# One fixed load order on the sync queue, modulation weights by halves, and attention heads transposed per 128 tokens as each is ready

## Chip, cores, metric

One Trainium2 chip; the kernel runs on one of its cores. The metric is the device time of one execution in microseconds (us): the median of three runs, and beside it one profiled execution of its own.

## What is computed

A slice of a diffusion backbone with two layers over 256 latent tokens and 256 context tokens, width 1024, all in float32. Every layer takes six modulation vectors from a conditioning vector (6 x 1024 columns of `mod_w` per layer), mixes tokens, normalises, sends the tokens through a grouped mixture of 16 experts (two chosen per token) and normalises again. Layer 0 mixes by differential attention, layer 1 by pooling:

```python
ml = (jax.nn.silu(c) @ mod_w[i] + mod_b[i])[:, None, :]
sh1, sc1, g1, sh2, sc2, g2 = jnp.split(ml, 6, axis=-1)
hl = xl * (1.0 + sc1) + sh1
# layer 0, per block of 128 query tokens, 8 heads, two score maps per head
s = jnp.einsum('bqhnd,bkhnd->nbhqk', qb, k) * scale
p = jax.nn.softmax(s, axis=-1)
a = p[0] - lam_full * p[1]
o = jnp.einsum('bhqk,bkhe->bqhe', a, v)
o = o * lax.rsqrt(jnp.mean(jnp.square(o), axis=-1, keepdims=True) + LN_EPS)
yl = (o * subln * (1.0 - lam_init)).reshape(B, Lq, D_MODEL) @ wo
xl = deepnorm_update(xl, yl, g1, ln_g[i, 0], ln_b[i, 0])
y2 = moe_ffn(tokens, router_w, router_b, moe_wg[i], moe_wu[i], moe_wd[i])
xl = deepnorm_update(xl, y2, g2, ln_g[i, 1], ln_b[i, 1])
```

## The kernel before, in words

The program is written out by hand for every engine; semaphores order it. Each engine, and each of the queues that issue loads, works through its own list in order.

**Memory.** The largest buffer is `ring`: ten slots of 128 x 4096 floats, 2 MB each. An expert takes six slots (two each of `moe_wg`, `moe_wu`, `moe_wd`), and the ring is refilled in the order of FREE while experts run. Before the experts the same slots hold weights of the attention, tokens, keys, values, queries and heads. A unit is 2 MB of weights, 1024 x 512.

**Ahead of the experts.** PHASE_A is the order in which PE uses its units: four modulation units ("mod", 0, 2, 1, 3), then ("k", j), ("q", j), ("v", j) for two halves j of the heads, then ("wo", 0) and ("wo", 1). `half_group` (first half of the contraction, then second) and `group` multiply one of twenty groups of GROUPS; groups 10 to 19, those of j = 1, come one per attention step through FILL.

The other twenty modulation units (SUMS, NSUM = 20) are summed on DVE: `unit_sum(n)` is two calls of `half_sum`, eight instructions that multiply a 128x512 piece by a column of the conditioning and add it into `sums` (the first L1269, six L1271, the last L1273). They pass through ring slots 2 and 3 in turn. EARLY_SUMS = 8 units are summed before the first attention step, with `rope_batch` (L1307 to L1310) before unit 6 and after unit 7; STEP_SUMS = 10 come one per step, the last two behind the attention. `row_batch(b)` on PE (L592) takes four finished sums.

**Steps.** There are NS = 16 attention steps, one per (half j, 128 tokens t, head h) in STEPS. In step s PE multiplies a filling group (s = 1 to 9), does the scores of step s (`scores`, L685), turns the weights of step s-2 (`turn_probs`, L538) and multiplies values of step s-3 (`values`, L703). DVE takes the maximum of the scores (L1391, L1392), combines the two maps of the step before (L1397, L1398, L1402), and sums a unit. ACT does the exponentials (L1096), copies the turned weights (L1100) and the results (L1105, L1107). PE waits in `scores(s)` for the exponentials of s-1, and these wait for DVE's maximum.

**Heads.** After the steps DVE normalises the heads of each 128 tokens (`norm_heads(t)`, L1322 to L1329) between two ACT pieces, `heads_std(t)` (L1077, a square root) and `copy_heads(t)` (L1084); between these PE turns the heads (`turn_heads(t)`, L538), and then multiplies by the output weights (`project(t, h)`, L722). `job(3)`, `job(4)` (L744) and `row_batch(4)` stand among them. Then come the first normalisation and the routing, and the experts begin (L862).

**Queues.** The sync queue (SP; every load is at L414) carries the attention weights and after them the experts' units. Its list waits for what frees a slot: `load_early` by FREED_BY, `slot_free(v)` for the first ten experts' units. The modulation units of SUMS come through the queue of GpSimd (POOL, L518), 2 MB at a time:

```python
for n, (layer, m) in enumerate(SUMS):
    s = 2 + n % 2
    if n < 2:
        pool.wait_ge(sem("unit_used"), s - 1)
        pool.wait_ge(sem("early_loaded_6"), 16)
    else:
        pool.wait_ge(sem("summed"), n - 1)
    pool.dma_start(slot(s), mod_w[layer, m]).then_inc(sem(f"sum_loaded_{n % 2}"), 16)
```

ACT's own queue swaps halves of keys and queries for the rotation (L1034, eight loads of 128 KB from ring to ring per half j).

## Time and profile before

| | us |
|---|---|
| runs (3) | median 1250.11, lowest 1246.59, highest 1251.18 |
| profiled execution | 1251.67 |
| its span | 1249.8 |
| PE busy | 1139.6 (91%) |
| DVE busy | 357.7 (29%) |
| ACT busy | 165.4 (13%) |
| POOL busy | 15.9 (1%) |

The span runs from the first to the last recorded instruction; the profiled execution took 1.87 us more than it. All positions below are microseconds from the start of the span. PE runs the matmuls, PEld its weight loads, DVE the vector work, ACT the activations; a name with q (SPq, ACTq) is a queue that issues loads. The loads themselves run on 16 DMA engines, which moved 480.17 MB, 384 GB/s in the mean. The program writes every float32 matmul as one instruction and the profile counts two.

### The profile page before, as it was taken

The numbers are of one execution on the slowest core, as the hardware profiler recorded it, in microseconds if no ns is written. First come the engines' busy times: TensorE is split into PE (matmuls) and PEld (weight loads), VectorE is DVE, ScalarE is ACT, GpSimd is POOL, SyncE is SP. The second block draws the span as 40 slices with busy tenths as digits, with TensorE's granted clock in tenths as the row PEclk, the third lists the DMA queues.
The fourth block names the chain that finished last, engine by engine and source line by source line (L and its number), as shares of the span: only waits on it lengthen the run. The fifth ranks groups of instructions, "written<-read, shape, count | busy, mean of one in ns | idle before, by whom it ended". The sixth has DMA issues, their size and how long they took to land.

```text
span 1249.8 us, 12318 instructions
## 1 busy us (share of the span) xinstructions
PE 1139.6 (91%) x5288; PEld 510.1 (41%) x5288; DVE 357.7 (29%) x729; ACT 165.4 (13%) x398; POOL 15.9 (1%) x28
## 2 busy tenths in 40 slices
PE   8995998888999999999999898899999999999995
PEld 3552464535444334333333336543333334333331
DVE  1458889764111112111111104211111111111113
ACT  1110223524100001000000003301000000100000
POOL 0000000000000000000000001000000000000000
PEclk9997999789999999999999999899999999999998
DMA  9997596937799999999999999799999999999993
GB/s 395 403 337 256 216 329 268 394 145 303 318 429 427 428 428 427 428 427 427 427 428 428 427 420 426 311 428 427 427 429 428 427 427 428 427 427 428 428 427 156
DMA packets 37273, 480.17 MB, mean 384 GB/s; under 512 B 4704, under 2 KB 5984, under 8 KB 8032
## 3 DMA queue, kind: packets, MB, share of 16 engines
q1 hardware_dynamic: 33280, 434.96, 82.7%
q0 software_dynamic: 2880, 41.94, 8.9%
q10 hardware_dynamic: 1056, 2.43, 0.6%
q8 instruction: 44, 0.72, 0.2%
q14 instruction: 13, 0.11, 0.0%
HBM read 476.18 MB, written 1.05 MB: 382 GB/s over the span
## 4 chain that ended last, share of the span: by engine, by line
PE 70%; DVE 14%; DMA 11%; issue 3%; ACT 2%; SPq 0%; DVEq 0%; POOLq 0%
PE ps L862 51%; DMA ring<-in_mod_w 7%; PE ps L854 5%; PE ps L870 5%; DMA ring<-in_moe_wu 3%; DVE ring L1271 3%; PE ps L722 2%; DVE work L1594 2%; DVE modp L1271 1%; DVE work L1598 1%; PE ps L878 1%; DVE extra L1271 1%; DVE small L1391 1%; PE ps L622 1%; PE ps L538 1%
## 5 line engine op out<-in xcount | busy, mean ns | idle before, releaser
L862 PE MATMUL ps<-ring,tra 128*64 128x512 f32 x2048 | 446.7, 594 | 2.2 <-ACT tra L1149 1.1
L862 PEld LDWEIGHTS ps<-ring,tra 128*64 128x64 f32 x2048 | 145.9, 137 | 298.1 <-issue 294.0
L862 PE MATMUL ps<-ring,work 128*64 128x512 f32 x1024 | 228.5, 598 | 29.2 <-DVE work L1594 29.2
L862 PEld LDWEIGHTS ps<-ring,work 128*64 128x64 f32 x1024 | 83.2, 137 | 153.8 <-issue 117.4
L1589 DVE TENSOR_TENSOR work<-ps,work 128x512 f32<-128x512 f32 x32 | 22.1, 692 | 277.8 <-ACT work L1156 277.8
L1156 ACT ACTIVATE work<-ps 128x512 f32<-128x512 f32 x32 | 19.1, 597 | 535.1 <-PE ps L862 535.1
L870 PE MATMUL ps<-work,extra 64*128 64x512 f32 x256 | 63.6, 615 | 21.0 <-DVE work L1598 21.0
L1149 ACT ACTIVATE tra<-ps,cols 128x128 f32<-128x128 f32 x128 | 48.2, 456 | 245.3 <-PE ps L854 245.3
L854 PEld LDWEIGHTS ps<-extra,xn 128*128 128x128 f32 x512 | 63.8, 203 | 25.7 <-issue 22.7
L1592 DVE TENSOR_TENSOR work<-work,ps 128x512 f32<-128x512 f32 x32 | 22.0, 688 | 181.4 <-PE ps L862 181.4
L854 PE MATMUL ps<-extra,xn 128*128 128x128 f32 x512 | 69.5, 293 | 2.7 <-DVE extra L1502 2.7
L622 PE MATMUL ps<-ring 128*128 128x512 f32 x128 | 58.2, 609 | 0.7 <-ACT ring L1045 0.7
L870 PEld LDWEIGHTS ps<-work,extra 64*128 64x128 f32 x256 | 22.0, 186 | 61.4 <-DVE work L1598 46.3
L1598 DVE TENSOR_TENSOR work<-ps,gt 128x512 f32<-128x512 f32 x16 | 11.1, 692 | 117.0 <-PE ps L862 117.0
L1598 DVE TENSOR_TENSOR work<-ps,rows 128x512 f32<-128x512 f32 x16 | 11.1, 691 | 115.3 <-PE ps L862 115.3
L622 PEld LDWEIGHTS ps<-ring 128*128 128x128 f32 x128 | 24.5, 195 | 33.6 <-issue 33.5
L1594 DVE COPY work<-ps 128x512 f32<-128x512 f32 x32 | 22.1, 692 | 50.8 <-PE ps L878 50.8
L1271 DVE SCALAR_TENSOR_TENSOR ring<-ring,cols 128x512 f32<-128x512 f32 x48 | 36.1, 752 | 1.7
L1096 ACT ACTIVATE work<-ps,small 128x512 f32<-128x512 f32 x32 | 21.7, 683 | 72.6 <-DVE small L1392 72.6
L628 PE MATMUL ps<-ring 128*128 128x256 f32 x128 | 30.1, 396 | 1.3 <-DMA ring<-in_attn_wqkv 1.3
L625 PE MATMUL ps<-ring 128*128 128x512 f32 x64 | 28.1, 592 | 0.0
L563 PE MATMUL ps<-cst 128*128 128x512 f32 x44 | 23.7, 670 | 4.3 <-DMA cst<-in_consts 4.0
(186 smaller groups left out, 752.4 us busy)
## 6 DMA issues: line engine op xcount, KB each, us to landing
ring<-in_moe_wg SPq DMA_DIRECT2D x64, 2048.0 KB, 25.0
ring<-in_moe_wu SPq DMA_DIRECT2D x64, 2048.0 KB, 23.4
ring<-in_moe_wd SPq DMA_DIRECT2D x64, 2048.0 KB, 23.1
ring<-in_mod_w POOLq DMA_DIRECT2D x20, 2048.0 KB, 9.6
ring<-in_mod_w SPq DMA_DIRECT2D x4, 2048.0 KB, 18.4
ring<-in_attn_wqkv SPq DMA_DIRECT2D x4, 2048.0 KB, 13.8
ring<-in_attn_wo SPq DMA_DIRECT2D x2, 2048.0 KB, 10.6
ring<-in_tokens SPq DMA_DIRECT2D x2, 1024.0 KB, 16.2
```

What stands on the lines that cost most here:

```text
L563: mm(bank(bk), ident, cst[:, 0:NB], start=True, stop=True, skip_group_check=True)
L622: return mm(bank(acc_bank(g)), w[:, k, t * P:t * P + P], hT[:, k, :], start=first, stop=end)
L625: return mm(bank(acc_bank(g)), hT[:, k, t * P:t * P + P], rhs, start=first, stop=end)
L628: last = mm(bank(acc_bank(g), 0, P, n * TOK, (n + 1) * TOK), w[:, k, hd * P:hd * P + P], hT[:, k, 0:TOK], start=first and n == 0, stop=end ...
L722: last = mm(bank(2 * t + h), oT[t][:, k, :], wo[:, k, :], start=(k == 0), stop=(k == KT - 1))
L854: last = mm(bank(bk, 0, P, k * P, k * P + slots), xn[:, c0:c0 + P], sgat[:, t, 0:slots], start=(t == 0), stop=(t == TT - 1), skip_group_ch ...
L862: last = mm(ps[SLOTS * h:SLOTS * h + SLOTS, b, :], lhs(k0 + k), w[:, k, h * NB:(h + 1) * NB], start=(k0 + k == 0), stop=(k0 + k == KT - 1) ...
L870: last = mm(bank(2 * t + h), sw[SLOTS * h:SLOTS * h + SLOTS, t * P:t * P + P], ysb[SLOTS * h:SLOTS * h + SLOTS, :], start=False, stop=True ...
L1149: nc.scalar.activation(xg[i // 2 % 2][:, kk, :], bank(bk, k * P, k * P + P), ACT.Identity, bias=one(bcol[2 * layer], kk, 1), scale=one(aco ...
L1271: link(v_.scalar_tensor_tensor(out=acc, in0=w[:, k, :], scalar=ck, in1=acc, op0=ALU.mult, op1=ALU.add))
L1594: v_.tensor_copy(work[:, NB:2 * NB], bank(7)).then_inc(sem("hTt_copied"), 1)
L1598: v_.tensor_tensor(ysb, bank(6), gt[layer], ALU.mult).then_inc(sem("ys_ready"), 1)
```

## The change

The SP queue gets one list, LOADS, for all weights ahead of the experts: an integer n is unit n of SUMS, loaded as two 1 MB halves; a pair is an attention unit; "rows" the router's weights and the bias rows; "x" the latent tokens. Each half waits for the sum of the same half two units earlier (the semaphore half_summed takes the place of summed). The POOL queue loads nothing any more. DVE waits per half. On DVE and ACT the heads of the first 128 tokens are normalised inside the last steps (s = NS-1 and NS+1), and PE turns them right behind `turn_probs(NS - 1)`; it turns those of the second 128 tokens ahead of `project(0, 1)`, with `job(4)` and `row_batch(4)` behind it.

```diff
+LOADS = [("q", 0), 0, 1, ("v", 0), 2, "rows", 3, 4, ("k", 1), 5, 6, 7, 8, ("q", 1), 9, 10, 11, 12, ("v", 1), 13, 14, ("wo", 0),
+         15, 16, 17, ("wo", 1), "x", 18, 19]
...
-            for unit in EARLY:
+            for unit in (("mod", 0), ("mod", 2), ("k", 0), ("mod", 1), ("mod", 3)):
                 load_early(unit)
...
+            def load_sum_unit(n):
+
+                layer, m = SUMS[n]
+                for half in range(2):
+                    if n >= 2:
+                        sp.wait_ge(sem("half_summed"), 2 * (n - 2) + half + 1)
+                    else:
+                        early_used(sp, ("mod", (0, 2)[n]))
+                    c0, c1 = half * UNIT // 2, (half + 1) * UNIT // 2
+                    load(slot(2 + n % 2)[:, c0:c1], mod_w[layer, m][:, c0:c1], sem(f"sum_loaded_{n % 2}_{half}"))
+
+            for what in LOADS:
+                if what == "rows":
+                    load_rows()
+                elif what == "x":
+                    load(xn[:, :].rearrange("p (t n) -> p t n", t=TT), x[0].rearrange("(t p) n -> p t n", p=P), sem("x_loaded"))
+                elif isinstance(what, tuple):
+                    load_early(what)
+                else:
+                    load_sum_unit(what)
...
                 elif v in (6, 7):
-                    sp.wait_ge(sem("summed"), NSUM - 7 + v)
+                    sp.wait_ge(sem("half_summed"), 2 * (NSUM - 7 + v))
...
-            for n, (layer, m) in enumerate(SUMS):
...
-                pool.dma_start(slot(s), mod_w[layer, m]).then_inc(sem(f"sum_loaded_{n % 2}"), 16)
...
                     values(NS - 3)
                     turn_probs(NS - 1)
+                    turn_heads(0)
                     values(NS - 2)
                     values(NS - 1)
                     job(3)
-                    turn_heads(0)
                     project(0, 0)
-                    job(4)
...
-            project(0, 1)
-            row_batch(4)
             pe.wait_ge(sem("aT_copied"), NS)
             pe.wait_ge(sem("o_copied"), NS)
             turn_heads(1)
+            project(0, 1)
+            job(4)
+            row_batch(4)
...
+                if s == NS - 1:
+                    heads_std(0)
                 if 2 <= s < NS + 2:
                     act.wait_ge(sem("aT_done"), s - 1)
                     nc.scalar.copy(aT[s % 2], bank(4)).then_inc(sem("aT_copied"), 1)
+                if s == NS + 1:
+                    copy_heads(0)
...
-                if half == 0:
-                    dve.wait_ge(sem(f"sum_loaded_{n % 2}"), 16 * (n // 2 + 1))
-                    if n >= SUM_BUFS:
-                        dve.wait_ge(sem("row_done"), (n - SUM_BUFS) // BATCH + 1)
+                dve.wait_ge(sem(f"sum_loaded_{n % 2}_{half}"), 16 * (n // 2 + 1))
+                if half == 0 and n >= SUM_BUFS:
+                    dve.wait_ge(sem("row_done"), (n - SUM_BUFS) // BATCH + 1)
...
-            norm_heads(0)
+                if s == NS - 1:
+                    norm_heads(0)
```

The SP queue behind the first units, before (`unit_used` counts units that PE is done with; 128x4096 is 2 MB, 128x2048 is 1 MB):

```order
L414 DMA cols<-in_attn_subln 128x1
L414 DMA ring<-in_attn_wqkv 128x4096 [waits unit_used]
L414 DMA xn<-in_attn_wqkv 128x2048
L414 DMA tra<-in_attn_wqkv 128x2048
L414 DMA rwa<-in_router_w 128x256
L414 DMA rb<-in_router_b 128x16
L414 DMA rows<-in_bias_rows 128x512 x2
L414 DMA pscale<-in_scale_rows 128x512
L414 DMA ring<-in_attn_wqkv 128x4096 [waits unit_used] x3
L414 DMA ring<-in_attn_wo 128x4096 [waits unit_used] x2
L414 DMA xn<-in_x 128x2x1024
L414 DMA ring<-in_moe_wg 128x4096 [waits unit_used]
```

And the same queue with the change, up to the loads behind ("q", 1):

```order
L417 DMA ring<-in_attn_wqkv 128x4096 [waits unit_used]
L417 DMA ring<-in_mod_w 128x2048 [waits unit_used] x4
L417 DMA xn<-in_attn_wqkv 128x2048
L417 DMA tra<-in_attn_wqkv 128x2048
L417 DMA ring<-in_mod_w 128x2048 [waits half_summed] x2
...
L417 DMA ring<-in_mod_w 128x2048 [waits half_summed] x4
L417 DMA ring<-in_attn_wqkv 128x4096 [waits unit_used]
L417 DMA ring<-in_mod_w 128x2048 [waits half_summed] x8
L417 DMA ring<-in_attn_wqkv 128x4096 [waits unit_used]
L417 DMA ring<-in_mod_w 128x2048 [waits half_summed] x8
```

The modulation halves now stand between the attention weights, and ("k", 1) behind the halves of unit 4.

PE at the end of the attention, before, from `values(NS - 2)` (the first L703 row) to the second projection of the first 128 tokens:

```order
L703 MATMUL ps<-ring,tra 128x128 [waits o_copied,qkv_out,aT_copied]
L703 MATMUL ps<-ring,tra 128x128 x3
L744 MATMUL ps<-rows,cst 128x512
L538 MATMUL ps<-cst,ring 128x128 [waits job_out,o_normed]
L538 MATMUL ps<-cst,ring 128x128 x7
L722 MATMUL ps<-ring,work 128x512 [waits oT_copied,early_loaded_1]
L722 MATMUL ps<-ring,work 128x512 x7
L744 MATMUL ps<-rows,cst 128x512 [waits job_out]
L722 MATMUL ps<-ring,work 128x512 [waits oT_copied,early_loaded_0]
L722 MATMUL ps<-ring,work 128x512 x7
```

And with the change, from `turn_heads(0)` on (L538 of ring are heads, L718 values, L737 the projections, L759 the jobs):

```order
L553 MATMUL ps<-cst,ring 128x128 [waits job_out,o_normed]
L553 MATMUL ps<-cst,ring 128x128 x7
L718 MATMUL ps<-ring,tra 128x128 [waits o_copied,qkv_out,aT_copied]
L718 MATMUL ps<-ring,tra 128x128 x3
...
L759 MATMUL ps<-rows,cst 128x512
L737 MATMUL ps<-ring,work 128x512 [waits oT_copied,early_loaded_1]
L737 MATMUL ps<-ring,work 128x512 x7
L553 MATMUL ps<-cst,ring 128x128 [waits o_normed,o_copied,aT_copied]
L553 MATMUL ps<-cst,ring 128x128 x7
L737 MATMUL ps<-ring,work 128x512 [waits oT_copied,early_loaded_0]
L737 MATMUL ps<-ring,work 128x512 x7
L759 MATMUL ps<-rows,cst 128x512 [waits job_out]
```

Both turns of heads moved up by one block of other PE work, and a job moved down.

## Rows read from the trace of the kernel before

**Rows 1.** Windows in the experts: window, busy us of each engine (instructions), clock, DMA share, GB/s
```profile
405.00:465.00 60.00, 58.10 (x282) 22.95 (x280) 9.94 (x21) 4.80 (x11) 0.00 (x0) 1.00 1.01 428
```
**Rows 2.** Waits of the SP queue, 285 to 345 us: total us, times, longest
```profile
SPq L414 <- PE ps L862: 45.8, 6, 26.5
```
**Rows 3.** Window between last load ahead of the experts and first refill, columns as rows 1
```profile
312.00:316.00 4.00, 3.44 (x20) 2.77 (x21) 1.36 (x7) 2.55 (x7) 0.00 (x0) 0.79 0.00 0
```
**Rows 4.** Chain that ended last, 0 to 330 us, shares by line
```profile
by line: DMA ring<-in_mod_w 27.6%; DVE ring L1271 9.7%; PE ps L722 9.2%; DVE modp L1271 5.5%; PE ps L862 4.2%; DVE extra L1271 4.2%; issue 3.6%; DVE small L1391 3.6%; PE ps L622 2.6%; PE ps L703 2.3%; PE ps L685 2.2%; PE ps L854 2.0%; PE ps
```
**Rows 5.** Timeline of DVE, 44 to 115 us: start, duration, what, [idle before <-releaser]
```profile
44.16 0.14 DVE L1299 TENSOR_SCALAR cols<-cols 128x1 f32<-128x1 f32 x1
...
89.02 0.49 DVE L1269 TENSOR_SCALAR ring<-ring,cols 128x512 f32<-128x512 f32 x1 [13.73 <-DMA ring<-in_mod_w]
...
99.37 0.49 DVE L1269 TENSOR_SCALAR ring<-ring,cols 128x512 f32<-128x512 f32 x1 [4.36 <-DMA ring<-in_mod_w]
...
108.82 0.48 DVE L1269 TENSOR_SCALAR ring<-ring,cols 128x512 f32<-128x512 f32 x1
...
114.73 0.48 DVE L1269 TENSOR_SCALAR ring<-ring,cols 128x512 f32<-128x512 f32 x1
```
**Rows 6.** Timeline of PE, 43 to 125 us
```profile
43.42 8.86 PE L628 MATMUL ps<-ring 128*128 128x256 f32 x32 [1.32 <-DMA ring<-in_attn_wqkv]
...
101.42 7.03 PE L622 MATMUL ps<-ring 128*128 128x512 f32 x16
120.77 1.93 PE L592 MATMUL ps<-ring,cst 128*32 128x512 f32 x8 [12.32 <-DVE ring L1273]
124.30 2.08 PE L685 MATMUL ps<-ring 64*128 64x512 f32 x4 [1.60 <-DVE ring L1310]
```
**Rows 7.** Timeline of PE in the steps: scores of steps 1, 2 and 10
```profile
134.87 1.13 PE L685 MATMUL ps<-ring 64*128 64x512 f32 x4
...
143.00 1.13 PE L685 MATMUL ps<-ring 64*128 64x512 f32 x4
...
214.28 1.13 PE L685 MATMUL ps<-ring 64*128 64x512 f32 x4
```
**Rows 8.** Timeline of DVE in the steps: maxima of 1, 2, 4, 10, and unit 12
```profile
136.05 1.23 DVE L1391 TENSOR_REDUCE small<-ps 128x2 f32<-128x1024 f32 x1 [2.21 <-PE ps L685]
...
144.41 1.22 DVE L1391 TENSOR_REDUCE small<-ps 128x2 f32<-128x1024 f32 x1
...
162.14 1.23 DVE L1391 TENSOR_REDUCE small<-ps 128x2 f32<-128x1024 f32 x1 [0.29 <-PE ps L685]
...
168.61 0.49 DVE L1269 TENSOR_SCALAR ring<-ring,cols 128x512 f32<-128x512 f32 x1 [3.94 <-DMA ring<-in_mod_w]
...
223.34 1.22 DVE L1391 TENSOR_REDUCE small<-ps 128x2 f32<-128x1024 f32 x1
```
**Rows 9.** Windows by the queues at work, columns as rows 1
```profile
11.00:22.00 11.00, 10.75 (x54) 4.54 (x46) 3.10 (x8) 1.76 (x4) 0.00 (x0) 1.00 0.99 418
...
66.00:98.00 32.00, 32.00 (x98) 16.66 (x97) 14.64 (x21) 3.58 (x7) 1.58 (x3) 1.00 0.99 325
```
**Rows 10.** Timeline of POOL: the first two loads of modulation units
```profile
34.26 1.25 POOL L518 DMA_DIRECT2D ring<-in_mod_w  x2 [33.80 <-DMA ring<-in_mod_w]
```
**Rows 11.** Timeline of ACT behind the steps: loading the square root's table
```profile
252.27 1.28 ACT L1077 ACT_TABLE_LOAD   x1
```
**Rows 12.** Timeline of PE behind the steps: projections, and the first expert
```profile
257.91 9.37 PE L722 MATMUL ps<-ring,work 128*128 128x512 f32 x16 [0.87 <-ACT work L1084]
...
278.04 13.97 PE L722 MATMUL ps<-ring,tra 128*128 128x512 f32 x32 [1.01 <-ACT tra L1084]
...
315.17 13.95 PE L862 MATMUL ps<-ring,tra 128*64 128x512 f32 x64 [0.56 <-ACT tra L1149]
```
**Rows 13.** Loads by kind, 0 to 300 us: count, KB each, median us to landing
```profile
cols<-in_cond SPq DMA_DIRECT2D x1, 8.0 KB, 2.7
```
**Rows 14.** Timeline of DVE behind the steps: normalising the first 128 tokens' heads
```profile
254.05 1.23 DVE L1329 TENSOR_TENSOR ring<-ring,small 128x1024 f32<-128x1024 f32 x1
```

More of the change, by code:

```diff
@@ L436, in load_early @@
                         load(slot(s)[:, c0:c1], src[:, c0:c1], sem("first_half_loaded" if part == 0 else f"early_loaded_{s}"))
-            for unit in EARLY:
+            for unit in (("mod", 0), ("mod", 2), ("k", 0), ("mod", 1), ("mod", 3)):
                 load_early(unit)
-                if unit == ("mod", 3):
-                    load(small9[:, 0:512], rope, sem("attn_small_loaded"))
-                    load(lamb, attn_lam[0].rearrange("a b -> (a b)").partition_broadcast(P), sem("attn_small_loaded"))
-                    load(subln, attn_subln.rearrange("a n -> n a"), sem("attn_small_loaded"))
-                if unit == ("v", 0):
-                    load(rw[:, :], router_w, sem("router_loaded"))
-                    load(rb[:, 0:NE], router_b.partition_broadcast(P), sem("router_loaded"))
-                    for i in range(DEPTH):
-                        load(rows[i][:, :], bias_rows[i], sem(f"rows_loaded_{i}"))
-                    load(pscale[:, :], scale_rows, sem("pscale_loaded"))
@@ L450, in _, with load_rows @@
-            load(xn[:, :].rearrange("p (t n) -> p t n", t=TT), x[0].rearrange("(t p) n -> p t n", p=P), sem("x_loaded"))
+            load(small9[:, 0:512], rope, sem("attn_small_loaded"))
+            load(lamb, attn_lam[0].rearrange("a b -> (a b)").partition_broadcast(P), sem("attn_small_loaded"))
+            load(subln, attn_subln.rearrange("a n -> n a"), sem("attn_small_loaded"))
+            def load_rows():
+                load(rw[:, :], router_w, sem("router_loaded"))
+                load(rb[:, 0:NE], router_b.partition_broadcast(P), sem("router_loaded"))
+                for i in range(DEPTH):
+                    load(rows[i][:, :], bias_rows[i], sem(f"rows_loaded_{i}"))
+                load(pscale[:, :], scale_rows, sem("pscale_loaded"))
@@ L510, in _ @@
         def _(pool):
-            for n, (layer, m) in enumerate(SUMS):
-                s = 2 + n % 2
-                if n < 2:
-                    pool.wait_ge(sem("unit_used"), s - 1)
-                    pool.wait_ge(sem("early_loaded_6"), 16)
-                else:
-                    pool.wait_ge(sem("summed"), n - 1)
-                pool.dma_start(slot(s), mod_w[layer, m]).then_inc(sem(f"sum_loaded_{n % 2}"), 16)
             pool.wait_ge(sem("job_out"), JOBS.index("joint_1") + 1)
@@ L584, in row_batch @@
             def row_batch(b):
-                pe.wait_ge(sem("summed"), BATCH * b + BATCH)
+                pe.wait_ge(sem("half_summed"), 2 * (BATCH * b + BATCH))
                 if b == SUMS0 // BATCH:
@@ L1107, in _ @@
                     nc.scalar.copy(osb[:, t, hh * P:hh * P + P], bank(5, 0, P)).then_inc(sem("o_copied"), 1)
-            for t in range(TT):
-                heads_std(t)
-                copy_heads(t)
+            heads_std(1)
+            copy_heads(1)
             def std(n, t):
@@ L1268, in half_sum @@
                     if k == 0:
-                        link(v_.tensor_scalar(acc, w[:, 0, :], ck, None, ALU.mult))
-                    elif k < KT - 1:
-                        link(v_.scalar_tensor_tensor(out=acc, in0=w[:, k, :], scalar=ck, in1=acc, op0=ALU.mult, op1=ALU.add))
-                    else:
-                        v_.scalar_tensor_tensor(out=acc, in0=w[:, k, :], scalar=ck, in1=acc, op0=ALU.mult, op1=ALU.add)\
-                            .then_inc(sem("summed"), 1)
+                        ins = v_.tensor_scalar(acc, w[:, 0, :], ck, None, ALU.mult)
+                    else:
+                        ins = v_.scalar_tensor_tensor(out=acc, in0=w[:, k, :], scalar=ck, in1=acc, op0=ALU.mult, op1=ALU.add)
+                    if k % 4 < 3:
+                        link(ins)
+                ins.then_inc(sem("half_summed"), 1)
+                if half == 0:
+                    dve.wait_ge(sem("half_summed"), i + 1)
             def unit_sum(n):
```

## The prediction

> **What bounds the kernel now.** I read the experts first, because they are most of the span. There PE is busy for 58.10 of 60 us while the loads run at 428 GB/s [rows 1]; PE sets the pace and the loads keep up. What matters for a change ahead of the experts is whether PE finds the ring full when it begins. It does: between 312 and 316 us nothing is loaded at all [rows 3], and the SP queue's longest wait there, 26.5 us, is for PE to give a slot back [rows 2]. The last slots to be filled come free with the output projections, at a fixed distance ahead of the first expert, so they move with it. From the first expert at 315.17 us [rows 12] everything is the same chain of work whenever it starts. So the change is worth the time by which that start moves, one for one.
>
> Next I read the chain of waits up to 330 us. Loads of `mod_w` are its largest part, 27.6%, with the sums on DVE behind them [rows 4]. The timelines show where it bites. Between units 3 and 4 of the sums DVE stood 13.73 us for a load, before unit 5 another 4.36, and before unit 12, in the steps, 3.94 [rows 5, 8]. PE had all its early groups done at 101.42 + 7.03 = 108.45, then stood 12.32 us for the eighth sum and 1.60 for the rotation behind it, and began the scores at 124.30 [rows 6]. From there to the maximum of step 10 at 223.34 DVE is the slower of the two: PE had those scores ready from 214.28 on [rows 7, 8].
>
> **The first 108 us.** The change removes twenty POOL loads of 2 MB and adds forty SP loads of 1 MB. What counts is when they land. An issue took 0.6 us of a sequencer (two took 1.25 [rows 10]); forty of them, 25 us, are spread over 170 us in a queue that waits most of that time, and I cost them at nothing. For the rate I take 420 GB/s, near the 418 of a stretch in which the SP queue was alone, several of its loads being of 1 MB [rows 9]: 5.0 us for 2 MB, 2.5 for a half. The last early unit had landed at 33.8 [rows 10]; with the small loads behind it the list begins to land at about 35. It then goes: q0 40, unit 0 45, unit 1 50, v0 55, unit 2 60, the small rows (0.9 MB) 62, unit 3 67, unit 4 72, k1 with ACT's eight swaps (1 MB) beside it 79.5, units 5, 6, 7 at 84.5, 89.5, 94.5.
>
> On DVE a sum takes 114.73 - 108.82 = 5.91 us, and 108.82 - 99.37 - 5.91 = 3.54 is a rotation [rows 5]. It is free at 44.3 [rows 5] and needs only first halves to start: units 0 and 1 end at 56.1, unit 2 starts with its first half at 57.5 and ends 63.4, unit 3 70.4, unit 4 76.3; unit 5 starts at 82 and ends 87.9, rotation 91.4, unit 6 97.4, unit 7 103.3, rotation 106.8. PE meanwhile gains the 1.32 us that it stood for q0 [rows 6] and has its groups done at 107.1; the four matmuls of `row_batch(1)` take 1.1 (1.93 at the lower clock [rows 6]). The scores begin at **108.2** instead of 124.30, **16.1 us** earlier, and now PE is last, by about 1 us only. If that cover is gone, each further microsecond on DVE counts in full.
>
> **The steps.** PE came out of its idle time slow: four score matmuls took 2.08 us where later ones took 1.13, and the step took 10.57 us (124.30 to 134.87) against 8.13 for the next (to 143.00) [rows 6, 7]. Without the idle time I give the first step 8.1: scores of step 1 at 116.3, their maximum 1.2 later at 117.5. From the maximum of step 1 to that of step 10 DVE took 223.34 - 136.05 = 87.3 us, of it 3.94 for unit 12's load and 0.29 for PE [rows 8]. Without the load wait 83.4 remain: step 10 at **200.9, 22.4 us** earlier. PE alone needs at most 214.28 - 134.87 = 79.4 [rows 7], which is 195.7, so DVE stays last.
>
> The new waits in the list do not bite here by this schedule. ("v", 1) waits for k1, which PE is done with at about 133, as DVE frees the last half of unit 12 at 134; DVE wants unit 13, behind it, in step 5, near 158. ("wo", 0) waits for q1, done near 153; unit 15 behind it is wanted near 178. ("wo", 1) waits until about 192, and behind it stand x, units 18 and 19, wanted behind the steps, and the first experts.
>
> **Behind the steps.** Before, ACT's table load began at 252.27, DVE's normalisation at 254.05, and the projection at 257.91 [rows 11, 12, 14]: 5.6 us with no other work on PE but job(3). Now ACT loads the table (1.28) in the last step, ahead of a copy that PE waits for, and DVE's 1.23 and two small ones stand ahead of the last weights. They push PE's last values by 1.5 to 2.9 us, and turning heads inside the sequence costs PE 1.1 or more. I work out 3.1 us added against 5.6 removed: 2.5 gained. The second turning is followed by other PE work, which saves the 1.01 us at 278.04 [rows 12]. Job(4), moved behind a projection, needs 0.7 us on DVE, hidden by `row_batch(4)`. Together **3.5 us**. The ends: 0, if ACT's and DVE's new work lies wholly on the path, and 5.8, if PE is also at the higher clock in the first projection (9.37 for it against 13.97 for two [rows 12]).
>
> **Sum.** 22.4 + 3.5 = 25.9 us off the profiled execution's 1251.67 gives 1225.8. The median of the runs was 1.56 lower: **1224.2**.
>
> **Rivals.**
>
> 1. *The rate stays low.* From 66 to 98 us the DMA engines were 99% busy and moved 325 GB/s, with three queues at work [rows 9]. If the cause is not the mixture of queues, it remains. The 18.7 MB from v0 to unit 7 then take 57.5 us from 50, the last half lands at 107.5, and 3.0 + 3.5 + 0.3 later the scores begin at 114.3: 6.1 us less gained, 1230.3. For it: ACT's swaps remain. Against it: 418 and 428 with one queue [rows 1, 9]. The Trainium skill, page DMA: Bandwidth & Descriptors, section Issuing engines are not separate DMA queues, says that loads from any engine run on the same 16 DMA engines and interleave, so merging queues would change order and not rate; by that rule the sum is this rival's. The rows bear it out only in part, since no stretch shows these loads on one queue.
>
> 2. *Part of the waits remains.* The list is in order, and one late weight holds all halves behind it. Half of DVE's 22.0 us of load waits [rows 5, 8] staying would give 1235.2. Against it are the margins above, except the 1 us at 108.2.
>
> 3. *Slower: halves do not overlap.* If each load waited for the one before to complete, a half would cost its 2.5 us and the 2.7 us that a small load took alone [rows 13], a unit 10.4. The place is the SP queue ahead of the steps and in them. Up to unit 7: 35 + 8 x 10.4 + 10.4 (v0) + 7.7 x 2 (q0, k1) + 15.7 (five small ones) = 159.7, then 6.8 on DVE: scores at 166.5, 42 later. In the steps, ten units and four weights take 134.8 against 99.0, another 36. With the 3.5 this is 1325. It decides where a unit takes longer than a step of 8.36 [rows 8], or 1.7 us lost per half. Against it: 418 GB/s in a stretch with 1 MB loads queued [rows 9]. The Trainium skill, page SBUF — State Buffer, section The DMA setup-cost knee, speaks against this change: every transfer pays roughly 2 us whatever its size, so transfers should be as large as they can be. With that figure a unit would be estimated at 9.0, still over a step; queued loads in the rows do not show it.
>
> 4. *Nothing moves*, if something unseen holds the steps; PE's 12.32 us of idle time speaks against it.
>
> **How the numbers follow.** Forecast 0.62; rival 1 0.20; rival 2 0.10; rival 3 0.03; rival 4 0.03; more than forecast 0.02. A measurement can tell 0.5%, 6.3 us, from no change. Forecast, rivals 1 and 2 and the surplus are faster by more: 0.94, same 0.03, slower 0.03. The range goes down by the tail's 2.3 us and 3.5 of spread (a run stood that far from the median) to 1218, and up past rival 1 with nothing gained behind the steps (1233.8) to 1236.
>
> **What would show it.** Right: POOL issues no loads; DVE waits little for loads but some 5 us before unit 5; PE goes without a long gap from 107 to the scores at about 108; the maximum of step 10 near 201, the first expert near 289; nothing loading just ahead of it. The rate from 66 to 98 us separates rival 1. A load wait of over 3 us on DVE in the steps would show rival 2, halves landing 5 us apart rival 3. A first expert at 289 with a total above 1235 would prove the reading of the experts wrong.

## The result, and the profile after

The changed kernel took 1230.09 us, the median of 4 runs (1228.50 to 1231.78), and the kernel before 1249.60 (4 runs, 1246.59 to 1251.18). The ratio is 0.984 (0.9823 to 0.9857), so the change gains 19.5 us where 25.9 were forecast for it. The profiled execution took 1231.51 us, 20.2 less than the 1251.67 before.

The page of the changed kernel, its parts 1 and 3: the span, busy time of each engine, and the DMA queues (packets, MB, share of 16 engines).

```profile
span 1229.7 us, 12356 instructions
...
PE 1134.5 (92%) x5288; PEld 507.5 (41%) x5288; DVE 357.7 (29%) x729; ACT 165.7 (13%) x398; POOL 5.2 (0%) x8
...
q1 hardware_dynamic: 39040, 476.91, 93.2%
q10 hardware_dynamic: 1056, 2.43, 0.6%
```

POOL's queue is gone from the list. What SP issues (q1) is all but ACT's few small loads (q10), the swaps among them.

Now the same places as in [rows 5]: the timeline of DVE, 66 to 105 us (start, duration, what, and in brackets the idle time before it and its releaser). The line that scales a unit by its column is now 1286.

```profile
66.50 0.49 DVE L1286 TENSOR_SCALAR extra<-ring,cols 128x512 f32<-128x512 f32 x1 [1.68 <-DMA ring<-in_mod_w]
...
74.95 0.49 DVE L1286 TENSOR_SCALAR ring<-ring,cols 128x512 f32<-128x512 f32 x1 [1.69 <-DMA ring<-in_mod_w]
...
88.71 0.49 DVE L1286 TENSOR_SCALAR ring<-ring,cols 128x512 f32<-128x512 f32 x1 [6.54 <-DMA ring<-in_mod_w]
...
104.06 0.48 DVE L1286 TENSOR_SCALAR ring<-ring,cols 128x512 f32<-128x512 f32 x1
```

The 13.73 us wait of [rows 5] is gone and unit 4 starts at 74.95 instead of 89.02. A quarter of that lead is lost again at unit 5, which waits 6.54 us and starts at 88.71 instead of 99.37. The timeline of PE, 98 to 126 us, to be laid beside [rows 6], shows who was waiting:

```profile
98.40 7.03 PE L637 MATMUL ps<-ring 128*128 128x512 f32 x16
...
110.11 1.94 PE L607 MATMUL ps<-ring,cst 128*32 128x512 f32 x8 [4.68 <-DVE ring L1288]
...
113.64 2.08 PE L700 MATMUL ps<-ring 64*128 64x512 f32 x4 [1.59 <-DVE ring L1329]
...
124.59 1.13 PE L700 MATMUL ps<-ring 64*128 64x512 f32 x4
```

PE's early groups end at 98.40 + 7.03 = 105.43. It then stands 4.68 us for the eighth sum (12.32 before) and 1.59 for the rotation. The scores begin at 113.64 instead of 124.30. That the groups end 1.7 us sooner than the forecast's 107.1 is a matter of PE's clock: the thirty-two matmuls that took 8.86 us behind the 1.32 us wait for q0 [rows 6] take 7.15 now that there is no wait (granted clock 0.51 from 44 to 46 us before, 1.00 now).

```profile
42.11 7.15 PE L643 MATMUL ps<-ring 128*128 128x256 f32 x32
```

After its idle time ahead of the scores PE is as slow as before the change (2.08 us for four matmuls, 1.13 later), and the first step takes 124.59 - 113.64 = 10.95 us.

The maxima of steps 1, 4 and 10 on DVE, which answer to [rows 8]:

```profile
125.76 1.23 DVE L1410 TENSOR_REDUCE small<-ps 128x2 f32<-128x1024 f32 x1 [2.59 <-PE ps L700]
...
151.85 1.23 DVE L1410 TENSOR_REDUCE small<-ps 128x2 f32<-128x1024 f32 x1 [0.28 <-PE ps L700]
...
209.29 1.22 DVE L1410 TENSOR_REDUCE small<-ps 128x2 f32<-128x1024 f32 x1
```

DVE waits for no load in the steps any more; step 1 to step 10 takes 83.53 us. Last, PE behind the steps, which answers to [rows 12]:

```profile
242.13 7.03 PE L737 MATMUL ps<-ring,work 128*128 128x512 f32 x16
...
258.68 14.00 PE L737 MATMUL ps<-ring,tra 128*128 128x512 f32 x32
...
295.84 13.95 PE L877 MATMUL ps<-ring,tra 128*64 128x512 f32 x64 [0.56 <-ACT tra L1167]
```

The first projection takes 7.03 us instead of 9.37, and the first expert begins 19.33 us earlier. The whole table, with the times of these rows in us:

| | before | forecast | after |
|---|---|---|---|
| unit 5 starts on DVE | 99.37 | 82 | 88.71 |
| PE's early groups done | 108.45 | 107.1 | 105.43 |
| scores of step 0 | 124.30 | 108.2 | 113.64 |
| maximum of step 1 | 136.05 | 117.5 | 125.76 |
| maximum of step 10 | 223.34 | 200.9 | 209.29 |
| first expert | 315.17 | about 289 | 295.84 |

Windows of the changed kernel say why unit 5 was late. The columns are those of [rows 1].

```profile
44.00:50.00 6.00, 6.00 (x28) 4.90 (x27) 5.72 (x11) 2.11 (x4) 0.00 (x0) 1.00 1.01 426
50.00:66.00 16.00, 16.00 (x46) 8.46 (x45) 11.77 (x17) 2.59 (x8) 0.00 (x0) 1.00 1.02 413
66.00:74.00 8.00, 8.00 (x29) 5.18 (x28) 5.75 (x8) 1.17 (x2) 0.00 (x0) 1.00 1.03 322
74.00:82.00 8.00, 8.00 (x25) 3.11 (x24) 5.58 (x8) 0.59 (x1) 0.00 (x0) 1.00 1.03 332
82.00:90.00 8.00, 8.00 (x20) 3.60 (x19) 1.41 (x3) 0.59 (x1) 0.00 (x0) 1.00 0.99 366
...
288.00:292.00 4.00, 2.63 (x15) 2.53 (x16) 2.12 (x13) 0.00 (x0) 0.00 (x0) 0.77 0.00 0
```

Up to 66 us the one queue moves 413 to 426 GB/s, most of it in halves of 1 MB. From 66 to 90 it is 322 to 366, though the DMA engines are as busy as before. In this stretch lie ACT's first eight swaps, and k1 (2 MB) stands in the list there. The last row shows that the ring is still full ahead of the experts. From 66 to 90 us 8.16 MB were moved (8 us at each of the three rates), which at the 423 GB/s of 50 to 58 us would take 19.3 us. So some 4.7 us are missing there, beyond what the swaps' own bytes need. The other 2.0 of the 6.7 us by which unit 5 is late were there before: unit 3 starts at 66.50 and was forecast to start at 64.5, with the landing of its first half.

### The profile page after: what moved, and what is told of

The parts are those of the page before. It is cut to its first block, busy times and chain, and to the rows that moved or that the text cites. A ratio compares the mean times of both kernels' runs of the same rounds, so it can differ in the third digit from the quotient of the medians.

```text
span 1229.7 us, 12356 instructions
## 1 busy us (share of the span) xinstructions
PE 1134.5 (92%) x5288; PEld 507.5 (41%) x5288; DVE 357.7 (29%) x729; ACT 165.7 (13%) x398; POOL 5.2 (0%) x8
## 3 DMA queue, kind: packets, MB, share of 16 engines
HBM read 476.18 MB, written 1.05 MB: 388 GB/s over the span
## 4 chain that ended last, share of the span: by engine, by line
PE 81%; DVE 9%; DMA 6%; ACT 2%; issue 2%; DVEq 0%; ACTq 0%
PE ps L877 52%; PE ps L869 5%; PE ps L885 5%; DMA ring<-in_moe_wd 3%; PE ps L637 3%; DMA ring<-in_mod_w 3%; PE ps L737 2%; PE ps L640 2%; DVE work L1614 2%; DVE work L1618 1%; DVE ring L1288 1%; PE ps L700 1%; PE ps L893 1%; PE ps L643 1%; PE ps L578 1%
## 5 line engine op out<-in xcount | busy, mean ns | idle before, releaser
L637 PE MATMUL ps<-ring 128*128 128x512 f32 x128 | 58.6, 612 | 0.7 <-ACT ring L1060 0.7
L1288 DVE SCALAR_TENSOR_TENSOR ring<-ring,cols 128x512 f32<-128x512 f32 x56 | 42.1, 752 | 3.2 <-DMA ring<-in_mod_w 1.3
L1288 DVE SCALAR_TENSOR_TENSOR extra<-ring,cols,extra 128x512 f32<-128x512 f32 x42 | 31.6, 752 | 2.7 <-DMA ring<-in_mod_w 1.3
L1288 DVE SCALAR_TENSOR_TENSOR modp<-ring,cols,modp 128x512 f32<-128x512 f32 x42 | 31.6, 752 | 1.5
```

The costliest lines, as they stand in the source:

```text
L637: return mm(bank(acc_bank(g)), w[:, k, t * P:t * P + P], hT[:, k, :], start=first, stop=end)
L1288: ins = v_.scalar_tensor_tensor(out=acc, in0=w[:, k, :], scalar=ck, in1=acc, op0=ALU.mult, op1=ALU.add)
```

## The experiments

Two theories at first. **A**: ACT's swaps (sixteen loads of 32 partitions, 128 KB each) pull the rate of the other queue down while they run, and k1, beside them, puts the loss ahead of unit 5. **B**: the rate falls for another cause (the size of the loads, the addresses, the list), and the swaps happen to lie there.

### 1. The swaps left out

```diff
-                if t == (1 if kind == "q" else 3):
-                    act.wait_ge(sem("qkv_out"), g + 1)
-                    for n in range(4):
-                        to, of = 32 * n, 32 * (n ^ 1)
-                        load(swapped[b][to:to + 32], raw[b][of:of + 32], f"swapped_{b}")
...
-                dve.wait_ge(sem(f"swapped_{kind}"), 64 * (j + 1))
-                link(v_.tensor_tensor(swapped[kind], swapped[kind], sin, ALU.mult))
+                link(v_.tensor_tensor(swapped[kind], raw[kind], sin, ALU.mult))
```

> The sixteen swaps of ACT's queue are left out; the rotation multiplies the unswapped keys and queries instead, so queries and keys are not rotated properly. Theory A (the swaps of 1 MB slow every load beside them): from 66 to 82 us the rate rises from the 322 and 332 GB/s of the changed kernel to 400 or more, the wait for unit 5 on DVE falls from 6.54 us to under 2, the scores of step 0 begin at 108 to 109 instead of 113.64, and the time falls by 5 to 8 us, to about 1224. Theory B (the low rate has another cause, the swaps cost only the 2.5 us of their own bytes): the rate there stays under 370, scores begin at 111 or later, the time falls by at most 3 us, to 1227 or more.

Measured: 1218.18 us (5 runs, 1216.75 to 1221.62), ratio to before 0.9768 (0.9743 to 0.9792). Windows, columns as above, and the first scores of this kernel:

```profile
66.00:74.00 8.00, 8.00 (x27) 4.96 (x27) 7.64 (x12) 0.98 (x2) 0.00 (x0) 1.00 1.04 432
74.00:82.00 8.00, 8.00 (x25) 3.08 (x24) 4.72 (x7) 0.59 (x1) 0.00 (x0) 1.00 0.99 414
```
```profile
105.70 1.13 PE L700 MATMUL ps<-ring 64*128 64x512 f32 x4
```

322 became 432, 332 became 414. PE doesn't wait for DVE any more, and the scores start at 105.70, at 1.13 us for four. Theory A holds; B, which left the rate low, falls. The time fell by 11.9 us where 5 to 8 were expected. The scores begin earlier than the 108 to 109 expected, and PE isn't slow in the first step either: the next scores stand at 113.82, 8.12 us on. The kernel lacks the swaps' waits too, so its time alone would prove little; the rate is what tells.

### 2. Units of 2 MB in the same single queue

```diff
-                for half in range(2):
-                    if n >= 2:
-                        sp.wait_ge(sem("half_summed"), 2 * (n - 2) + half + 1)
...
+                if n >= 2:
+                    sp.wait_ge(sem("half_summed"), 2 * (n - 2) + 2)
...
+                load(slot(2 + n % 2), mod_w[layer, m], sem(f"sum_loaded_{n % 2}_0"))
...
-                dve.wait_ge(sem(f"sum_loaded_{n % 2}_{half}"), 16 * (n // 2 + 1))
+                dve.wait_ge(sem(f"sum_loaded_{n % 2}_0"), 16 * (n // 2 + 1))
```

> The changed kernel, with its one queue and order, but every modulation unit as one load of 2 MB that waits for both halves of the sum two units before. If the halves carry part of the gain: DVE waits for whole units ahead of the steps, the scores of step 0 begin 3 to 8 us later than 113.64, the time is 1233 to 1238. If halves are worth nothing, since the queue is full anyway: within 1.5 us of the changed kernel, 1229 to 1232. If halves cost something by being small: faster than 1228.

Measured: 1234.90 us (6 runs, 1231.72 to 1235.37), ratio 0.9888 (0.9866 to 0.991). The first and the longest of DVE's load waits ahead of the steps:

```profile
45.90 0.49 DVE L1284 TENSOR_SCALAR modp<-ring,cols 128x512 f32<-128x512 f32 x1 [2.05 <-DMA ring<-in_mod_w]
...
92.06 0.48 DVE L1284 TENSOR_SCALAR ring<-ring,cols 128x512 f32<-128x512 f32 x1 [5.69 <-DMA ring<-in_mod_w]
```

DVE waits for five loads ahead of the steps, 18.3 us in all, against seven and 14.6 us in the changed kernel (both summed over its timeline from 44 us). The scores begin at 116.99 instead of 113.64 and the first expert at 299.35 instead of 295.84. Halving is worth 3.5 us in the traces and 5 in the medians. Halving does not slow the loads down, as rival 3 had it.

### 3. and 4. The heads: undone in the changed kernel, and alone in the one before

The first edit puts the four pieces back where they were; the second, on the kernel before, is the same with + and - exchanged. The part of PE:

```diff
                     turn_probs(NS - 1)
-                    turn_heads(0)
                     values(NS - 2)
...
                     job(3)
+                    turn_heads(0)
                     project(0, 0)
+                    job(4)
...
+            project(0, 1)
+            row_batch(4)
             pe.wait_ge(sem("aT_copied"), NS)
...
             turn_heads(1)
-            project(0, 1)
-            job(4)
-            row_batch(4)
```

> The changed kernel with the heads turned and normalised at the places of before. As predicted the heads' part is worth 3.5 us: 1233.6. As the two profiles read (91.83 us from step 10's maximum to the first expert before, 86.55 after) it is worth 5.3: 1235.4. If the part is hidden: 1230.

> The kernel before with the heads' part of the change alone (PE, ACT, DVE). Undoing it in the changed kernel cost some 5 to 7 us; if the parts simply add, the time is 5 to 6 us under the kernel before's, a ratio of 0.995 to 0.996. If it gains only because DVE reaches the end of the steps in another rhythm, less than 2 us.

Measured, undone: 1235.23 us (6 runs, 1234.59 to 1236.81), ratio to before 0.99 (0.988 to 0.992). Alone: 1241.94 us against 1249.45 (7 and 12 runs), ratio 0.9946 (0.9928 to 0.9965). The first projection with the heads undone:

```profile
243.47 9.31 PE L737 MATMUL ps<-ring,work 128*128 128x512 f32 x16 [0.87 <-ACT work L1099]
```

It is back at 9.31 us behind a wait. From the maximum of step 10 to the first expert it takes 91.83 us before and 91.70 with the heads undone, but 86.55 after and 86.08 with the heads alone. So this part gives 5.2 to 5.8 us, whatever the rest does, and the two parts of the change simply add. The 7.5 us of the medians with the heads alone are more than that. In its trace the scores began at 122.66 instead of 124.30, though nothing ahead of them was edited: so traces of kernels that are the same up to there can differ by 1.6 us.

### 5. and 6. k1 later in the list

Nothing is left out here: the swaps are as slow as ever, and only the order of the list differs. The first edit also moves the small rows (0.9 MB); the second moves k1 alone.

```diff
-LOADS = [("q", 0), 0, 1, ("v", 0), 2, "rows", 3, 4, ("k", 1), 5, 6, 7, 8, ("q", 1), ...
+LOADS = [("q", 0), 0, 1, ("v", 0), 2, 3, 4, 5, ("k", 1), 6, 7, "rows", 8, ("q", 1), ...
```
```diff
+LOADS = [("q", 0), 0, 1, ("v", 0), 2, "rows", 3, 4, 5, ("k", 1), 6, 7, 8, ("q", 1), ...
```

> Only LOADS is edited: the small rows go behind unit 7 and (k, 1) behind unit 5. If the end of the sums ahead of the steps is set by what lands before unit 5: the wait of 6.54 us goes, units 3 to 5 land 2 to 7 us sooner, the scores of step 0 begin at 107.5 to 110, and the time falls by 4 to 7 us, to about 1224 to 1226. If the bytes to unit 7 set it whatever their order: the wait moves to unit 6 or 7, scores at 113 to 114, 1230.

> LOADS with (k, 1) behind unit 5 and the rows where the change has them. Moving both gave scores at 106.30 instead of 113.64. If (k, 1) alone is the cause: scores at 106 to 108, time within 1.5 us of that run, 0.975 to 0.977 of the kernel before. If the 0.9 MB of rows, many of them in small packets, matter as much: scores at 109 to 111, 0.979 to 0.982.

Measured: 1218.16 us (5 runs, 1216.53 to 1220.94), ratio 0.9761 (0.9738 to 0.9784), for both moves; 1222.27 (5 runs), ratio 0.9786 (0.977 to 0.9802), for k1 alone. Windows of the kernel with both moves, and its first scores:

```profile
66.00:74.00 8.00, 8.00 (x29) 5.15 (x28) 6.62 (x10) 1.17 (x2) 0.00 (x0) 1.00 1.03 299
74.00:82.00 8.00, 8.00 (x25) 3.09 (x24) 5.75 (x8) 0.59 (x1) 0.00 (x0) 1.00 1.01 306
82.00:90.00 8.00, 8.00 (x20) 3.61 (x19) 6.50 (x7) 0.58 (x1) 0.00 (x0) 1.00 1.01 415
```
```profile
106.30 1.13 PE L700 MATMUL ps<-ring 64*128 64x512 f32 x4
...
114.42 1.13 PE L700 MATMUL ps<-ring 64*128 64x512 f32 x4
```

Beside the swaps the rate is even lower than after the change (299 and 306), and higher behind them (415 against 366), so from 66 to 90 us both kernels move the same, 340 GB/s in the mean. And yet the scores start at 106.30 and the first step takes 8.12 us, 0.6 us behind the kernel without swaps: the low rate costs hardly anything once the weight that PE doesn't want yet stands behind the unit that DVE does. With k1 alone moved PE still stands 1.96 us for the rotation, and takes 117.65 - 107.83 = 9.82 us for the step:

```profile
107.83 1.13 PE L700 MATMUL ps<-ring 64*128 64x512 f32 x4 [1.96 <-DVE ring L1329]
```

The gain over the changed kernel is 11.9 us with both moves and 7.8 with k1 alone in the medians, 10.3 and 6.8 in the first expert of the traces (285.53 and 289.04). The first is more than the 4 to 7 us expected. The second has its scores where "k1 alone is the cause" wanted them and its ratio between the two cases: k1 is the larger part. The rest is the rows'; the intervals of the two ratios overlap, so the 3.5 us between them are shown by the traces alone.

### 7. What in the swaps is slow

Each swap load reads 32 partitions of the ring and writes 32 others. Two edits take one property away each. The first replaces the four loads by one of 128 partitions with the same 512 KB; the second keeps the four but reads them from HBM.

```diff
-                    for n in range(4):
-                        to, of = 32 * n, 32 * (n ^ 1)
-                        load(swapped[b][to:to + 32], raw[b][of:of + 32], f"swapped_{b}")
+                    load(swapped[b], raw[b], f"swapped_{b}")
...
-                dve.wait_ge(sem(f"swapped_{kind}"), 64 * (j + 1))
+                dve.wait_ge(sem(f"swapped_{kind}"), 16 * (j + 1))
```
```diff
-                        load(swapped[b][to:to + 32], raw[b][of:of + 32], f"swapped_{b}")
+                        load(swapped[b][to:to + 32], tokens[of:of + 32, 0:1024].rearrange("p (h t) -> p h t", h=4), f"swapped_{b}")
```

> In the changed kernel the four loads of 32 partitions that swap keys or queries are replaced by one plain copy of the same 512 KB over all 128 partitions, so queries and keys are not rotated properly. If the form on 32 partitions, which reads and writes only a part of the ring's partitions at a time, makes the neighbours slow: the rate from 66 to 82 us is over 390, scores near 109 to 110. If any copy from SBUF to SBUF does: 320 to 340 as in the changed kernel, scores near 113.

> The changed kernel with its sixteen loads on 32 partitions, but each reads the same number of bytes from HBM (tokens) instead of the ring, so queries and keys are not rotated properly. If reading the ring on 32 partitions is what slows the neighbours: the rate from 66 to 82 us is 380 or more and the scores begin at 109 to 111. If writing on 32 partitions is enough: 300 to 350, scores near 113.

Measured: 1226.04 us for the one wide copy and 1228.10 for the reads from HBM (one run each, so the times don't tell them from the changed kernel's 1227.62 to 1230.09). The windows of 66 to 74 us do, the wide copy first:

```profile
66.00:74.00 8.00, 8.00 (x27) 4.96 (x27) 6.47 (x10) 0.99 (x2) 0.00 (x0) 1.00 1.03 426
```
```profile
66.00:74.00 8.00, 8.00 (x28) 4.98 (x27) 5.45 (x8) 1.14 (x2) 0.00 (x0) 1.00 1.02 308
```

With the same bytes beside it in one wide copy the rate stays at 426 (415 in the next 8 us), and the scores start at 108.92. Unit 5 on DVE shows the price of the narrow form, 88.71 - 84.00 = 4.71 us between the two traces:

```profile
84.00 0.49 DVE L1284 TENSOR_SCALAR ring<-ring,cols 128x512 f32<-128x512 f32 x1 [4.85 <-DMA ring<-in_mod_w]
```

Read from HBM in the narrow form the rate is 308 and 325, with the scores at 113.45. So it is the narrow form on the writing side, not the bytes nor the reading of the ring, that holds the other queue up. The wide copy is also one load where there were four; no run parts the number of loads from their width. The DMA view of 66 to 82 us of the changed kernel agrees:

```profile
q1 hardware_dynamic: 466, 4.33, 83.7%
q10 hardware_dynamic: 318, 0.90, 19.0%
```

The same view of the kernel with the wide copy:

```profile
q1 hardware_dynamic: 636, 5.67, 84.7%
q10 hardware_dynamic: 288, 1.05, 16.4%
```

In nearly the same share of the engines' time SP's queue moves 4.33 MB beside the narrow loads and 5.67 beside the wide one. It is slowed inside its share. The Trainium skill, page SBUF — State Buffer, section Door 1: The DMA port swizzle, says that 32 neighbouring partitions reach only half of SBUF's 16 ports, and page DMA: Bandwidth & Descriptors, section Back-pressure in remote DMA, that a saturated destination port stalls the other queues of the same DMA engine. The runs agree with both together; the second is told of another kind of transfer, and no run here looks at single ports.

### 8. Halves from POOL's queue

The first kernel meant for this lacks its edit and is the changed kernel itself. It doesn't test its expectation, which the second below does, and its time stands as a repeat:

> The changed kernel, but the modulation halves are issued by the POOL queue again, with the same waits for half sums; attention weights, rows and x stay on SP in their order. If the single order makes the gain: DVE waits over 10 us for loads before unit 5 or 4 again, the scores of step 0 begin at 117 to 124, time 1236 to 1243. If the halves make it: scores at 112 to 115, time 1228 to 1232.

Measured: 1227.62 us (5 runs, 1222.92 to 1232.03), ratio 0.9828 (0.9801 to 0.9855), the changed kernel once more. Then with the edit:

```diff
-                else:
-                    load_sum_unit(what)
...
+            for n, (layer, m) in enumerate(SUMS):
+                for half in range(2):
+                    if n >= 2:
+                        pool.wait_ge(sem("half_summed"), 2 * (n - 2) + half + 1)
...
+                    pool.dma_start(slot(2 + n % 2)[:, c0:c1], mod_w[layer, m][:, c0:c1])\
+                        .then_inc(sem(f"sum_loaded_{n % 2}_{half}"), 16)
```

> The changed kernel, but the modulation halves really come from the POOL queue, with the same waits for half sums; attention weights, rows and x stay on SP in their order. If one queue in one order carries the gain: loads of both queues share the DMA engines again, DVE waits over 10 us for loads ahead of unit 5, the scores of step 0 begin at 117 to 122, time 6 to 10 us over the changed kernel's. If the halves carry it: scores at 112 to 115 and a time within 2 us of the changed kernel's.

Measured: 1235.95 us (6 runs, 1232.85 to 1238.24), ratio 0.9894 (0.9876 to 0.9912). DVE's wait for unit 5, and PE ahead of the scores:

```profile
87.55 0.49 DVE L1294 TENSOR_SCALAR ring<-ring,cols 128x512 f32<-128x512 f32 x1 [7.69 <-DMA ring<-in_mod_w]
```
```profile
118.78 1.93 PE L615 MATMUL ps<-ring,cst 128*32 128x512 f32 x8 [10.14 <-DVE ring L1296]
```

DVE also waited 5.56 us in the unit ahead of that and 3.96 behind it, and PE stood 10.14 us. The scores began at 122.31, 8.7 us later than after the change. In the medians the one ordered queue is worth 6 to 8 us. From 50 to 66 us these two queues moved 388 GB/s, the single queue 413. The windows of the two queues from 66 us on:

```profile
66.00:74.00 8.00, 8.00 (x34) 6.12 (x33) 4.97 (x8) 1.17 (x2) 1.05 (x2) 1.00 1.02 377
74.00:82.00 8.00, 7.01 (x23) 2.67 (x22) 3.01 (x4) 0.58 (x1) 0.53 (x1) 1.00 1.02 315
82.00:90.00 8.00, 8.00 (x20) 3.48 (x19) 2.35 (x4) 0.58 (x1) 0.00 (x0) 1.00 1.02 333
90.00:98.00 8.00, 8.00 (x20) 3.61 (x19) 3.90 (x7) 0.58 (x1) 0.76 (x2) 1.00 1.00 343
```

Here the swaps are spread over a longer time. They moved 0.14 MB up to 74 us and 0.91 from there to 98; with one queue 0.90 of their 1.05 MB moved from 66 to 82 us. Where they run, the rate is about the same, 315 to 343 with two queues and 322 and 332 with one; from 66 to 98 us it is 342 in the mean with two and 354 with one. How much of the cost is the lost order and how much the lower rate ahead of it, this run doesn't part. In its trace the early loads were also some 2 us later already ahead of the edit's place, so 8.7 is an upper end for the scores.

### 9. A version that beats both

On top of the moved list, one sum fewer in the steps; it is done behind them, where PE is given its work so that it covers the sum.

```diff
-STEP_SUMS = 10
+STEP_SUMS = 9
...
+            project(1, 0)
             row_batch(4)
-            for h in range(2):
-                project(1, h)
+            project(1, 1)
...
-            for n in range(EARLY_SUMS + STEP_SUMS, NSUM):
+            for n in range(EARLY_SUMS + STEP_SUMS, NSUM - 1):
                 unit_sum(n)
             job_out(4)
+            unit_sum(NSUM - 1)
```

> A version meant to be faster: LOADS with (k, 1) behind unit 5 and the rows behind unit 7, as in the run before with that list; and nine sums in the steps instead of ten, three behind them, with row_batch(4) between the last two projections. With that list alone the maximum of step 10 stood at 199.12 and DVE was last in the steps. One sum less (5.91 us) on DVE: step 10's maximum at 195 to 196, where PE becomes last; time 3 us under that run, some 0.974 of the kernel before. Against it: if the third sum behind the steps delays the first normalisation, the same as that run, 0.976, or slower.

Measured: 1215.62 us (5 runs, 1214.77 to 1216.11), ratio 0.9733 (0.9713 to 0.9752). The maximum of step 10 on DVE, and the first expert on PE:

```profile
193.52 1.23 DVE L1410 TENSOR_REDUCE small<-ps 128x2 f32<-128x1024 f32 x1
```
```profile
278.81 13.95 PE L877 MATMUL ps<-ring,tra 128*64 128x512 f32 x64 [0.56 <-ACT tra L1167]
```

The maximum of step 10 is 5.60 us earlier than with the moved list alone (199.12), about the 5.91 of a sum, and the first expert 6.72 (285.53 there). The medians are 2.5 us apart and the intervals of the two overlap, so that this last step is faster is shown by the traces and only likely by the times. That it beats the changed kernel, by 12 to 14 us, is shown by both.

## Why the prediction was right in its direction and 5.9 us off in its size

**The reading of what bounds the kernel held.** The ring was full ahead of the experts (0 GB/s from 288 to 292 us). From the first expert to the end of the span it took 934.6 us before and 933.9 after, and between 933.6 and 934.3 in the kernels with k1 later, nine sums and the whole units. The start of the experts moved one for one into the time in each of them.

**Rate and landing times: the step that failed.** It is the term "k1 with ACT's eight swaps (1 MB) beside it 79.5". I gave the swaps the price of their bytes at 420 GB/s. Up to 66 us the figure was good (413 and 426 in the windows). On DVE the schedule had units 3, 4 and 5 start at 64.5, 70.4 and 82; they started at 66.50, 74.95 and 88.71, so 2.0, 4.6 and 6.7 us late. The 4.7 us that came behind unit 3 are the swaps' cost beyond their bytes, and the wide copy of experiment 7 gives them back (unit 5 at 84.00). The first 2.0 stay without a shown cause; they are there in the wide copy's kernel too (66.61). Rows for the low rate were there: 325 GB/s in the stretch in which the swaps lie [rows 9]. I put that down to the mixture of three queues and took its end for granted when POOL's was removed. Windows of 8 us of the kernel before give 406 and 366 GB/s ahead of its swaps (50 to 66 us) and 338, 327, 343 and 293 beside them. That is a reason to ask about the swaps and no proof, since the rate had begun to fall ahead of them.

**The first step.** "Without the idle time I give the first step 8.1" hung on the term above. PE had little cover at 108.2, as the prediction said (DVE was to be done at 106.8), so the 6.7 us of unit 5 arrived there as 5.4, and because PE then stood for 4.68 and 1.59 us, it was slow again and the step took 10.95. With k1 and the rows moved there was no idle time, and the step took 8.12. The term was right in its condition and the condition wasn't met: another 2.9 us. The clock was left out in the other direction as well: the forecast took only the wait of 1.32 us off PE's early groups, which were done 3.0 us earlier. That gave nothing, since DVE was last.

**The steps.** 83.4 us were forecast from the maximum of step 1 to that of step 10, and 83.53 measured; no wait for a load was left. None of the new waits in the list bit.

**Behind the steps.** 3.5 us forecast, between 0 and 5.8; 5.28 measured, 5.2 in the reversal, 5.8 alone. The upper end was near because PE did the first projection in 7.03 us, the case set aside for that end: its granted clock was 1.00 there, and 0.76 over the 9.37 us before.

**The sum.** 25.9, less 8.4 by step 10, plus 1.8 behind the steps gives 19.3, which is the 19.33 us by which the first expert moved; 0.8 more came in the experts, 20.1 in the span.

**The rivals.** Rival 1 came out nearly to the number: scores at 114.3 and 1230.3 us against 113.64 and 1230.09. Its mechanism is only half right, though. It had the rate low from 50 us on and "ACT's swaps remain" as one argument; low it was only beside the swaps, and only in their narrow form. The match of the total is luck: the slow first step (2.9 us), which the rival doesn't have, is nearly offset by what the heads gave beyond 3.5 us (1.8) and by the experts (0.8). The Trainium skill (DMA: Bandwidth & Descriptors, section Issuing engines are not separate DMA queues) says that loads from every engine run on the same 16 DMA engines and interleave. That merging queues then changes order and not rate agrees with the stretches in which the swaps run, 315 to 343 GB/s with POOL's queue and 322 and 332 without, and less with 50 to 66 us, where one queue moved 413 and two 388. Rival 2 (half the waits remain) had the right kind of loss at 1235.2, but the waits of the steps went wholly. Rival 3 is ruled out: halves of 1 MB moved at up to 426 GB/s and gained time. The Trainium skill's rule in SBUF — State Buffer, section The DMA setup-cost knee, that each transfer pays some 2 us, is not seen as lost time between loads that stand queued. Rival 4 fell with the first row.

**The parts.** By their own reversals, in the medians, the heads are worth 5.1 us, the halves 4.8 and the one queue 5.9. That is 15.8 of 19.5. Each of these three kernels was measured beside its own runs of the kernel before; as what is missing of the 19.5 us against those, the parts are 7.0, 6.7 and 6.3, which makes 20.0. So the missing 4 us are within the spread of the medians. Whether the parts give anything together that none gives alone is not shown (a whole unit in a second queue was not tried with the heads moved).

## What to carry to other kernels

A queue in a fixed order is only as good as its order: before giving a weight its place, ask which engine has no cover for being late there, and put every load that is not wanted yet behind that engine's next one; moving one such load gained more than splitting all the units (6.8 us against 3.5 in the traces). A transfer beside others is priced not by its bytes but by the total rate of the stretch in which it runs, so read that stretch in narrow windows and look at the shape of the small transfers before blaming the number of queues. And where an engine's idle time is to vanish, price the case in which a little of it stays: here 6 us of it cost another 3 in the step behind.

## What the runs showed of the hardware that was not expected

- Loads of 32 partitions that move 0.90 to 1.05 MB in 16 us took the total, 414 to 432 GB/s without them, down to between 273 and 335 from 66 to 82 us, in all eight traces with one queue that have them. One load of 128 partitions in place of four, with the same bytes, left it at 415 to 426. Whether the narrow ones read SBUF or HBM made no difference (322 and 308 from 66 to 74 us).
- Loads of 1 MB in one queue were as fast as loads of 2 MB: 426 GB/s from 44 to 50 us against 427 with whole units (experiment 2) and 428 in the experts [rows 1].
- PE's clock at the start of the steps. The windows of the changed kernel behind those shown above (columns as there), and one of the kernel with k1 and the rows moved:

```profile
104.00:110.00 6.00, 1.43 (x4) 0.36 (x2) 5.75 (x10) 0.65 (x2) 0.00 (x0) 0.93 1.01 388
110.00:114.00 4.00, 2.29 (x10) 0.56 (x12) 3.78 (x6) 0.00 (x0) 0.00 (x0) 0.50 0.95 408
114.00:118.00 4.00, 4.00 (x7) 1.32 (x6) 2.09 (x4) 0.70 (x3) 0.00 (x0) 0.50 1.01 426
118.00:125.00 7.00, 7.00 (x16) 2.85 (x16) 4.96 (x7) 1.06 (x5) 0.00 (x0) 0.90 0.60 184
```
```profile
106.00:110.00 4.00, 4.00 (x14) 1.55 (x11) 2.56 (x6) 1.05 (x4) 0.00 (x0) 1.00 0.97 410
```

  The granted clock was 1.00 (2.4 GHz) up to 104 us, fell to 0.50 (1.2 GHz) while PE stood for DVE (from 105.43 on), and was still 0.50 from 114 to 118 us with PE busy all the time. Without the idle time it stayed at 1.00. The waits of 4.68 and 1.59 us therefore cost 2.8 more in the step behind them (10.95 against 8.12). With k1 alone moved a wait of 1.96 us cost 1.7 (9.82).
